# A large fp32r kernel on one core: one memory area moved ahead of the halves of the normalized input

## What is computed

```python
def first_block(x, ...):
    h = rmsnorm(x, norm_g[l])
    proj = jnp.einsum('bsd,dn->bsn', h, w_in[l])          # 1024 x 12288
    a_u, a_v, a_z, b_p, b_z, c_h, c_b, c_c, c_z, gate_logits = jnp.split(proj, ...)
    ya = spatial_gating(...); yb = multiscale_pool(...); yc = c_b * causal_depthwise_conv(...) * silu(c_z)
    merged = gates[0] * (ya @ w_branch_a) + gates[1] * (yb @ w_branch_b) + gates[2] * (yc @ w_branch_c)
    x = x + merged @ w_out
    ...
def second_block(x, ...):
    # i = 0: p = rms_norm(x) @ ev_w_in; s5_layer, glu, conformer_conv; y = [ya, yb] @ ev_w_out
    # i = 1: p = rms_norm(x) @ od_w_in; gla_branch (4 heads, chunks of 64); y = ... @ od_w_out
    x = x + rms_norm(y, norm_post[i])
```

## Time and profile before

| | before |
|---|---|
| time, median of 3 runs | 1596.4 us (1595.74 to 1596.65) |
| the profiled execution, its own time | 1596.45 us |
| its span, first to last instruction | 1594.7 us |
| TensorE matmuls (PE) | 1577.0 us busy, 99%, 8985 instructions |
| weight loads (PEld) | 1374.2 us, 86% |
| VectorE (DVE) | 1163.5 us, 73% |
| ScalarE (ACT) | 730.1 us, 46% |
| GpSimd (POOL) | 206.4 us, 13% |
| HBM traffic | 132 GB/s over the span |
| granted TensorE clock | mean 0.998 of full speed |

### The profile page before, as it was taken

How to read it: one execution, slowest core, us unless ns; L and a number is a source line. 1 busy time by engine, 2 the same in 40 slices (tenths; PEclk the granted TensorE clock), 3 DMA queues, 4 the chain that set the end, 5 groups by cost and what they waited for, 6 DMA issues and landing times.

```text
span 1594.7 us, 22200 instructions
## 1 busy us (share of the span) xinstructions
PE 1577.0 (99%) x8985; PEld 1374.2 (86%) x8985; DVE 1163.5 (73%) x1542; ACT 730.1 (46%) x996; POOL 206.4 (13%) x241
## 2 busy tenths in 40 slices
PE   9999999999999999999999999999999899999998
PEld 7888888888998999888998889878888788988887
DVE  5267274667888898556999999984475868677677
ACT  5333242253541355345454554568255436455364
POOL 4991000000000000004223221122010000000000
PEclk9999999999999999999999999999999999999999
DMA  8664633231342333524978897698533123322241
GB/s 246 171 176 127 163 119 107 66 106 53 107 132 80 106 107 106 196 81 175 251 155 214 187 202 190 135 208 184 174 120 93 31 90 107 104 72 79 66 159 67
DMA packets 166635, 211.84 MB, mean 133 GB/s; under 512 B 52177, under 2 KB 102021, under 8 KB 165894
## 3 DMA queue, kind: packets, MB, share of 16 engines
q1 hardware_dynamic: 146725, 176.31, 35.6%
q0 software_dynamic: 18144, 31.99, 11.6%
q10 hardware_dynamic: 1664, 2.13, 0.5%
HBM read 193.63 MB, written 16.78 MB: 132 GB/s over the span
## 4 chain that ended last, share of the span: by engine, by line
PE 92%; DVE 3%; DMA 2%; ACT 2%; issue 0%; SPq 0%; DVEq 0%; ACTq 0%
PE PS L2988 58%; PE PS L3192 20%; PE PS L2966 3%; PE PS L3410 1%; PE PS L3065 1%; DMA WR<-in_ev_w_in_dram 1%; PE PS L3342 1%; PE PS L3244 1%; PE PS L3440 1%; PE PS L3175 1%; DMA WL<-in_ev_w_in_dram 1%; PE PS L3158 0%; PE PS L3416 0%; PE PS L3270 0%; PE PS L3143 0%
## 5 line engine op out<-in xcount | busy, mean ns | idle before, releaser
L1148 ACT ACTIVATE WH<-WR 128x1024 fp32r<-128x1024 f32 x160 | 169.6, 1061 | 419.0 <-PE PS L2988 366.5
L2988 PE MATMUL PS<-HH,WH 128*128 128x512 f32 x800 | 312.1, 390 | 0.8 <-ACT G L1237 0.4
L2988 PE MATMUL PS<-HL,WH 128*128 128x512 f32 x800 | 311.4, 389 | 0.0
L2988 PE MATMUL PS<-HH,WL 128*128 128x512 f32 x800 | 311.3, 389 | 0.0
L1821 DVE TENSOR_TENSOR WL<-WR,WH 128x1024 fp32r<-128x1024 f32 x104 | 138.4, 1339 | 219.0 <-ACT WH L1148 218.5
L1162 ACT ACTIVATE WHS<-WRS 128x1024 fp32r<-128x1024 f32 x112 | 117.6, 1057 | 179.0 <-PE PS L2988 71.4
L2988 PEld LDWEIGHTS PS<-HH,WH 128*128 128x128 f32 x800 | 150.2, 188 | 33.7 <-issue 2.1
L2988 PEld LDWEIGHTS PS<-HH,WL 128*128 128x128 f32 x800 | 150.2, 188 | 31.3
L2988 PEld LDWEIGHTS PS<-HL,WH 128*128 128x128 f32 x800 | 150.2, 188 | 30.8
L1830 DVE TENSOR_TENSOR WLS<-WRS,WHS 128x1024 fp32r<-128x1024 f32 x112 | 136.6, 1221 | 49.5 <-ACT WHS L1162 49.1
L2459 DVE SCALAR_TENSOR_TENSOR TMP<-CP,PRM,TMP 128x512 f32<-128x512 f32 x232 | 154.9, 741 | 0.0
(11 more groups left out here) (540 smaller groups left out, 3431.1 us busy)
## 6 DMA issues: line engine op xcount, KB each, us to landing
WR<-in_w_in_dram SPq DMA_DIRECT2D x56, 512.0 KB, 4.3
WRS<-in_w_in_dram SPq DMA_DIRECT2D x40, 512.0 KB, 4.2
WR<-in_ev_w_in_dram SPq DMA_DIRECT2D x24, 512.0 KB, 5.0
WL<-in_ev_w_in_dram POOLq DMA_DIRECT2D x24, 512.0 KB, 8.0
WRS<-in_od_w_in_dram SPq DMA_DIRECT2D x24, 512.0 KB, 4.2
WR<-in_od_w_in_dram SPq DMA_DIRECT2D x20, 512.0 KB, 4.2
WR<-in_ev_w_in_dram SPq DMA_DIRECT2D x32, 256.0 KB, 3.2
WR<-in_ev_w_out_dram SPq DMA_DIRECT2D x16, 512.0 KB, 4.8
```

Of the source, the lines that this page charges most:

```text
L1148: act.activation(WH[:, n % RING, :, :], WR[:, n % RING, :, :], ACT.Copy).then_inc(w_hi, 1)
L2988: mm = pe.matmul(out_banks[m], st, mv, start=(kt == 0 and i == 0), stop=(kt == 2 * per - 1 and i == 2))
```

## The change

The list of areas is written in another order. R1 stands directly behind WL, ahead of HH, HL, YH and YL. The total size stays the same, and every area from R2 on keeps its address. HH, HL, YH and YL move up by 17344 bytes and R1 moves down by 65536. Modulo 16384, R1 stays where it was, and HH, HL, YH and YL now start 960 bytes off WR, WH and WL, as R2 to R6 already do. No instruction is added, removed or moved on any engine; only addresses differ.

```diff
         region.top = start
-        for name, size in (("WR", 16384), ("WH", 16384), ("WL", 16384), ("HH", 16384), ("HL", 16384),
-                           ("YH", 16384), ("YL", 16384), ("R1", 17344), ("R2", 16384), ("R3", 16384),
+        for name, size in (("WR", 16384), ("WH", 16384), ("WL", 16384), ("R1", 17344), ("HH", 16384),
+                           ("HL", 16384), ("YH", 16384), ("YL", 16384), ("R2", 16384), ("R3", 16384),
                            ("R4", 16384), ("R5", 16384), ("R6", 8192), ("ident", 512), ("PRM", 4 * 8 * N_VEC),
```

## The result

The changed kernel takes 1618.73 us (median of 4 runs, 1618.11 to 1619.45), the kernel before beside it 1596.53 us. The ratio is 1.014, with a 95% interval of 1.0124 to 1.0156. It is slower by 22 us. The forecast was 1594.6 us, no change that can be told, with a range up to 1603.

What follows compares the result with a forecast made beforehand. TensorE, busy 99% of the span, bounds the kernel through start-to-start matmul distances. Terms -10.3 (256 columns) + 7.4 - 0.3 (input moving) + 2.1 (input standing) - 0.6 - 0.2 = -1.9 us, from 1596.45 to 1594.6 us; range 1586 to 1603.

Steps and rivals of the forecast that it cites:

- rival D: Whole kernel: placement does nothing, the differences belong to shape or neighbours; 1596.4 us, chance 0.08.
- rival E: First block: weights come too late for faster short matmuls, 6.5 us lost to VectorE waits; 1601 us, chance 0.04.
- the term of the 3360 long matmuls with the input moving: 512 columns, input halves moving, weights standing: 2.2 ns more each, +7.4 us, less 0.3 under transfers.
- the mirrored case (L3175, L3326): 512-column pieces with the standing operand 960 bytes off: 229.0 and 229.4 ns, taken as price for the opposite direction.
- the mixed piece with OH and OL: Weights moving, OH aligned and OL off standing: 231.2 ns, 4.4 over aligned, taken as upper bound for input moving.
- Rival C: Every section with the input moving: long matmuls cost 4.4 ns more instead of 2.2; 1601.7 us, chance 0.20.
- the -6.5 us of the 256 columns in the first block: First block's short matmuls, 672 and 1008: all at 0.1133 us each, saving 2.6 + 3.9 us.
- The heads' -3.8: Heads' 256-column matmuls with HH or G4H/G4L: 576 save 6.7 ns each, 3.8 us.
- OH and OL: Three pieces of 96 in the first three heads become uniform: 231.2 to 229.0 ns, -0.6 us.
- the standing input: 512 columns, weights moving, input halves standing: 948 matmuls at 2.2 ns more each, +2.1 us.
- a_in: 192 matmuls with a strided standing operand, 237.1 ns each: no change, 2 us either way.
- The rule quoted in the prediction: Skill's statement on engine ports, read as placement having no effect, time staying at 1596.4 us; prediction said rows contradict it.

Runs made afterwards that it cites:

- The run with the extra matmuls: The changed kernel with 8 more aligned 256-column matmuls ahead of block 1 in each of the first block's 10 jobs: 1622.23 us, ratio 1.0162.
- the run with 64 bytes: The kernel before with 64 unused bytes ahead of HH, its order of areas kept: 1611.59 us, ratio 1.0093.

## Why the prediction was wrong

**The method held.** TensorE is the bound before and after, no instruction moved, and the distances account for the result. Placement does act (rival D falls). The faster short matmuls of rival E never came in the kernel after, so it doesn't test E. The run with the extra matmuls had 168 in 19.07 us and no VectorE piece in the chain of either short section. But with the extra ones its second section is as long as before (120.0 us against 118.1), so the supply at the full faster pace stays untested.

**The step that failed is the term of the 3360 long matmuls with the input moving.** It was to be "2.2 ns, the value of the mirrored case (L3175, L3326), because at 256 columns the mirrored cases are equal". It measured 6.5 ns, +21.2 us in all instead of +7.1: 14 of the 23.5 us by which the sum was off. L3175 is d = -960, which is 64 modulo 512; the change makes d = +960, which is 448. These are different offsets with different prices, 229.0 and 233.3 ns, as the run with 64 bytes showed by exchanging them. Every long stretch of 512 columns at 448 or 960 with the input moving took 233.3 to within 0.2, while at 64 both values occur, so the smaller one can't be counted on even in its own direction. At 256 columns both happened to take 113.3 in the kernel before, and I made a rule of it. The prediction put the size between bounds of -6.7 and +4.4 ns, and the upper bound was too low: it was the mixed piece with OH and OL, d = 0 and 64, and a piece of other offsets is no bound on one that it doesn't contain. Rival C had the place right ("every section with the input moving") and the price at 4.4 ns. With 6.5 it gives 1594.6 + 3220 x 4.3 ns = 1608.4 us, a good half of the way from 1594.6 to 1618.7. Most of the remaining 10 us come from the 256 columns and from OH and OL, below.

**The second step that failed is the -6.5 us of the 256 columns in the first block**, which came out as +1.1. At d = 448 both 113.3 and 117.8 ns are steady rhythms. In the kernel before the blocks with S1H enter from the 120 ns rhythm of the aligned HH blocks and fall to 113.3; after, nothing is aligned, and all seven blocks stay at 117.8. The extra matmuls show it. The heads' -3.8 came out as -2.8: there the kernel after does get near 113.3 in places. The first two blocks of a head, HH and S1H, read 5.46/48 = 113.8 ns, against 5.62/48 = 117.1 in the kernel before:

```profile
1285.28 5.46 PE PS L3192 x48
```

**OH and OL** were to gain from agreeing and lost 0.6 us. Their d is 64 for all three products, which took 229.0 in L2966 of the same kernel, but they run at 22.40/96 = 233.3. With YH and YL alone off, OH and OL lie at the same offset to the weights, and the piece took 21.97/96 = 228.9. So at d = 64 there are two rhythms at 512 columns as well. The 96 matmuls at 1151.85 us above are another case: 233.3 ns behind YH and YL moving at 233.3, but 228.9 with HH and HL alone off, behind YH and YL at 226.8. Entry from a slow stretch is no rule, though, since the 96 ahead of L2966 in the kernel after follow one too and take 229.1. No experiment was made on what selects.

**Could the 233.3 at d = 448 be such a matter of history too?** The traces speak against it. The YH and YL piece behind the first short stretch took 44.79 or 44.80 us whether it was entered from 120 (only YH and YL off), from 117.8 (after) or from 113.5 (with the extra matmuls). Entered straight from aligned long matmuls at 226.7 it is 233.3 too: YH and YL at 256.4 us with YH and YL alone off, HH and HL at 305.5 us with HH and HL alone off. That is four entries, not all there are; no extra matmuls were put ahead of a stretch of 512 columns.

**The sums that held:** the standing input, +2.3 us (forecast +2.1), L3175 at 10.89 us (forecast 10.9), and a_in, +0.7 within the 2 us allowed. The first is partly luck, since 168 of its matmuls took 233.3 ns and not 229.0.

The rule quoted in the prediction, from the Trainium skill (SBUF - State Buffer, section "SBUF: two separate sides"), that PE never waits on anyone, says which engines wait for one another. It doesn't say that placement is without effect within TensorE, and the prediction's inference of 1596.4 us from it fails: 64 bytes of padding make the difference between 1601.8 and 1618.7 us. Whether that is waiting at a port no run shows.

What stays open is the mechanism below the numbers: why d = 64 can be a third as dear as 32 or 128, what picks a rhythm, and whether the period is 256 or 512 bytes.

## What to carry to other kernels

Where fp32r matmuls run back to back, read the distance from start to start by the offset of the moving from the standing operand, with its sign, and keep that offset at 0 modulo 512 bytes for the long ones (512 columns). Don't carry a price from +x to -x, or from one length of matmul to another, and don't take a mixed piece as the upper bound. When a group changes whose own addresses did not, look at what runs ahead of it: a steady rhythm can be inherited.

## What the runs showed of the hardware

- All of this is for fp32r matmuls with a weight load for each. At 512 columns, aligned operands give 226.8 ns from start to start, and every other offset tried costs 2.2 to 6.5 ns more. At 256 columns it is the other way about: aligned is the slowest, 120.0, and offsets give 113.3 to 119.
- In the first block's short sections, one and the same instruction sequence with the same addresses ran at 117.9 or 113.5 ns, by eight matmuls put ahead of it, and stayed so for 168 matmuls.
- At 512 columns the operands moving 64 bytes ahead (modulo 512) ran at 229.0 or 233.3 ns within one execution, with the choice not explained.
- 32 unused bytes ahead of the halves cost 1.7% of the whole kernel.
